# Inputs awaited one by one in five products, and two gate tiles moved into the waits of the attention

## The reference, cut to what matters

```python
def swiglu(x, w_in, w_out):
    gate, up = jnp.split(x @ w_in, 2, axis=-1)
    return (jax.nn.silu(gate) * up) @ w_out

def token_mixer(h, ...):
    z_hy, q, k, v, gates = jnp.split(h @ w_in, SPLITS, axis=-1)
    y_hy = hyena_branch(z_hy, ...) @ w_hy_out
    ...
    o = diff_attention(q, k, v, lam)
    o = rmsnorm(o, subln_g) * (1.0 - lam_init)
    y_da = o.reshape(B, L, D_ATTN) @ w_da_out
    g_hy, g_da = jnp.split(jax.nn.sigmoid(gates), 2, axis=-1)
    return (g_hy * y_hy + g_da * y_da) @ w_o
```

## Time and profile before

| | |
|---|---|
| time, median of 3 | 1986.11 us |
| the profiled execution | 1985.95 us, span 1984.1 us |
| PE busy | 1781.3 us (90%), granted clock 0.941 on average |
| DVE, ACT, POOL busy | 850.5, 310.7, 111.3 us |
| gates | 734.03 to 784.2 us |
| attention | to 859.9 us |
| head norm and `daout` | to 905.65 us |
| experts | from 1544.05 us |

### The profile page before, as it was taken

How to read it: one execution, slowest core, us unless ns; L and a number is a source line. 1 busy time by engine, 2 the same in 40 slices (tenths; PEclk the granted TensorE clock), 3 DMA queues, 4 the chain that set the end, 5 groups by cost and what they waited for, 6 DMA issues and landing times.

```text
span 1984.1 us, 29568 instructions
## 1 busy us (share of the span) xinstructions
PE 1781.3 (90%) x12188; PEld 1373.0 (69%) x12188; DVE 850.5 (43%) x1728; ACT 310.7 (16%) x707; POOL 111.3 (6%) x120
## 2 busy tenths in 40 slices
PE   6999999999999999999999999999999866666765
PEld 2788888888884878669999998888778321121212
DVE  4766666964442066734675236633433100000001
ACT  2200000010210112412111114212322100000000
POOL 2000000010100010000000002602001000000000
PEclk9999999999999999989999999989999887787778
DMA  8333444965442114116545863100359899999996
GB/s 362 131 130 129 137 136 158 353 219 193 149 149 85 64 57 157 43 64 234 186 167 172 292 215 115 43 23 24 130 219 395 348 433 432 427 431 431 433 433 291
DMA packets 46756, 426.08 MB, mean 215 GB/s; under 512 B 5331, under 2 KB 5940, under 8 KB 15548
## 3 DMA queue, kind: packets, MB, share of 16 engines
q1 hardware_dynamic: 37008, 386.97, 50.5%
q10 hardware_dynamic: 9644, 37.59, 5.3%
HBM read 423.49 MB, written 1.05 MB: 214 GB/s over the span
## 4 chain that ended last, share of the span: by engine, by line
PE 30%; DMA 19%; DVE 3%; POOL 2%; issue 1%; ACT 1%; SPq 0%; DVEq 0%; POOLq 0%; ACTq 0%
DMA arena<-experts_ring_dram 19%; PE bank L957 14%; PE bank L1132 6%; PE bank L1516 3%; PE bank L1800 2%; PE bank L1348 1%; DVE arena L2960 0%; PE bank L1619 0%; PE bank L1667 0%; PE bank L1398 0%; POOL rstd L868 0%; DVE rstd L2340 0%; PE bank L1710 0%; POOL arena L932 0%; PE bank L1593 0%
## 5 line engine op out<-in xcount | busy, mean ns | idle before, releaser
L957 PE MATMUL bank<-arena 128*128 128x256 f32 (+2 forms) x3296 | 624.8, 351 | 6.7 <-DVE arena L2811 1.9
L957 PEld LDWEIGHTS bank<-arena 128*128 128x128 f32 x3296 | 532.4, 192 | 92.0 <-issue 34.7
L1800 PE MATMUL bank<-arena 128*32 128x512 f32 x1400 | 230.3, 817 | 132.6 <-DMA arena<-experts_ring_dram 131.8
L1800 PEld LDWEIGHTS bank<-arena 128*32 128x32 f32 x1400 | 61.5, 143 | 294.7 <-issue 294.6
L1081 PE MATMUL bank<-arena 128*128 128x256 f32 x880 | 194.0, 379 | 0.0
L1081 PEld LDWEIGHTS bank<-arena 128*128 128x128 f32 x880 | 167.3, 190 | 22.9 <-issue 0.5
L1132 PE MATMUL bank<-arena 128*128 128x128 f32 x1512 | 169.2, 275 | 0.0
L1132 PEld LDWEIGHTS bank<-arena 128*128 128x128 f32 x1512 | 169.1, 192 | 0.1
L3151 DVE TENSOR_TENSOR arena<-arena,bank 128x512 f32<-128x512 f32 x8 | 5.5, 687 | 229.9 <-PE bank L1800 229.9
L2504 DVE SCALAR_TENSOR_TENSOR arena<-arena 128x1024 f32<-128x1024 f32 x56 | 68.4, 1221 | 0.0
L1516 PE MATMUL bank<-arena 64*64 64x64 f32 x2048 | 62.2, 221 | 0.8 <-POOL arena L932 0.5
(11 more groups left out here) (416 smaller groups left out, 1921.9 us busy)
## 6 DMA issues: line engine op xcount, KB each, us to landing
arena<-dense_dram SPq DMA_DIRECT2D x167, 1024.0 KB, 4.9
arena<-experts_ring_dram SPq DMA_DIRECT2D x41, 4096.0 KB, 26.9
arena<-ada_rest_dram ACTq DMA_DIRECT2D x56, 512.0 KB, 5.2
arena<-experts_dram SPq DMA_DIRECT2D x19, 1024.0 KB, 8.8
arena<-ada_head_dram SPq DMA_DIRECT2D x8, 1024.0 KB, 23.0
arena<-experts_dram SPq DMA_DIRECT2D x8, 512.0 KB, 9.8
arena<-tokens_dram ACTq DMA_DIRECT2D x1, 2048.0 KB, 20.0
arena<-experts_ring_dram SPq DMA_DIRECT2D x1, 2048.0 KB, 23.9
```

Source lines behind the costliest of these rows:

```text
L957: ins = mm(out, lhsT=w, rhs=rhs(k), start=k == 0, stop=k == k_tiles - 1)
L1800: ins = mm(ps[banks[half]][32 * e:32 * e + 32, :], lhsT=lhs[:, 2 * kp + par, CAP * e:CAP * e + CAP], rhs=slab[e][par][:, half * 512:half * ...
```

## The change

1. A `product` can be given a function `arrived`, called before each of its blocks. The first product of `ffn1_out` and of `ffn2_out` waits for all but the last two hidden tiles before block 0 and for these two before blocks 20 and 21. The first product of `daout` waits for bank k // 2 of the head norm before block k. `gated_add` counts every tile in `mix_ready`, and the first product of `wo` and of `wout` waits for tile k before block k. The waits for the whole input are gone.
2. Gate tiles 14 and 15, before the eighth pair, are plain products of 8 matmuls over 256 tokens. `gate14` stands behind the first scores, in bank 7; ACT copies it out after the first head's exponentials. `gate15` stands in bank 6 round the head norm: 2 blocks before the sums of squares, 5 between the sums and the spreading, 1 behind it. ACT applies both sigmoids after the head norm's root, and then loads the root's table again by a small Sqrt. DVE waits for them before tile 6 of `daout`.
3. The weight slabs are laid out in the new order; their number is unchanged.

```diff
-          ("uspec", {0: 2, 1: 2, 2: 2, 3: 2}), ("v_end", _rot(4)), ("yinv", _rot(8)), ("gates", _rot(16)),
-          ("att", {0: 8, 1: 8, 2: 8, 3: 8, 5: 8, 6: 8, 7: 8}), ("onorm", {5: 1, 0: 1, 1: 1, 2: 1, 3: 1}),
+          ("uspec", {0: 2, 1: 2, 2: 2, 3: 2}), ("v_end", _rot(4)), ("yinv", _rot(8)), ("gates", {0: 4, 1: 4, 2: 3, 3: 3}),
+          ("gate14", {7: 1}),
+          ("att", {0: 8, 1: 8, 2: 8, 3: 8, 5: 8, 6: 8, 7: 8}), ("gate15", {6: 1}), ("onorm", {5: 1, 0: 1, 1: 1, 2: 1, 3: 1}),
...
-GATE_PAIRS = KD
+GATE_PAIRS = KD - 1
+HY_EARLY = 2
...
+                    if arrived is not None:
+                        arrived(k)
...
-                pe.wait_ge(in_hid, FT)
...
-                pe.wait_ge(sv_hid, SEVENS)
...
+            def last_hidden(made):
+
+                def arrived(k):
+                    if k == 0:
+                        pe.wait_ge(made, FT - 2)
+                    elif k >= FT - 2:
+                        pe.wait_ge(made, k + 1)
+                return arrived
...
-            hyena_out(range(2))
+            hyena_out(range(HY_EARLY))
             scores(0)
-            hyena_out(range(2, 5))
+            take(pe, "gate14", 7, 0)
+            product(ps[7][:, 0:T], KD, lambda k: h1[:, k, 0:T], full[7])
+            hyena_out(range(HY_EARLY, 5))
...
+            def gate15(lo, hi):
...
+                for k in range(lo, hi):
+                    w, first = st.block()
+                    ins = mm(ps[6][:, 0:T], lhsT=w, rhs=h1[:, k, 0:T], start=k == 0, stop=k == KD - 1)
...
+            gate15(0, 2)
             pe.wait_ge(osq_ready, 8)
             take(pe, "onorm", 5, 0)
...
             ins.then_inc(full[5], 1)
+            gate15(2, 7)
             pe.wait_ge(hr_ready, 1)
...
-            for b in range(4):
-                evacuated(pe, "onorm", b, 0)
-            tiles("daout", KD, KD, lambda k: oT[:, k, :])
-            pe.wait_ge(mix_ready, 1)
...
+            gate15(7, KD)
+            for t in range(KD):
+                take(pe, "daout", t % 4, t // 4)
+                product(ps[t % 4][:, 0:T], KD, lambda k: oT[:, k, :], full[t % 4],
+                        arrived=None if t else lambda k: evacuated(pe, "onorm", k // 2, 0))
...
+            def mixed(stage):
+
+                return lambda k: pe.wait_ge(mix_ready, KD * stage + k + 1)
+
+            def second_hidden(k):
+                if k == 0:
+                    pe.wait_ge(sv_hid, SEVENS - 2)
+                elif k >= FT - 2:
+                    pe.wait_ge(sv_hid, SEVENS - FT + k + 1)
...
+            got(act, "gate14", 7, 0)
+            A(gates[:, 2 * GATE_PAIRS, :], ps[7][:, 0:T], ACT.Copy).then_inc(evac[7], 1)
...
+            got(act, "gate15", 6, 0)
+            A(gates[:, 2 * GATE_PAIRS + 1, :], ps[6][:, 0:T], ACT.Sigmoid).then_inc(evac[6], 1)
+            A(gates[:, 2 * GATE_PAIRS, :], gates[:, 2 * GATE_PAIRS, :], ACT.Sigmoid).then_inc(gate_done, 1)
+            A(fh[0:HEADS, 2 * T:2 * T + 1], eps[0:HEADS, 0:1], ACT.Sqrt)
...
-                    settle()
+                    if n == 0 and t == KD - 2:
+                        evacuated(dve, "gate15", 6, 0)
+                        dve.wait_ge(gate_done, GATE_PAIRS + 1)
+                    if t:
+                        dve.wait_ge(mix_ready, KD * n + t)
+                    else:
+                        settle()
                     tt_(rt[:, 0:T], ps[t % 4][:, 0:T], gts[:, first + t, :], mult).then_inc(evac[t % 4], 1)
                     evacuated(dve, stage, t % 4, t // 4)
-                    ins = tt_(dst[:, t, :], dst[:, t, :], rt[:, 0:T], add)
-                    if t < KD - 1:
-                        do(ins)
-                ins.then_inc(mix_ready, 1)
+                    tt_(dst[:, t, :], dst[:, t, :], rt[:, 0:T], add).then_inc(mix_ready, 1)
```

More of the change, by code:

```diff
@@ L63 @@
 N_COLS = _at
-DENSE = [("ffn1_in", FT), ("ffn1_out", 22), ("z", 12), ("qk", 8), ("v", 4), ("gates", 8),
-         ("hyout", 4), ("daout", 4), ("wo", 8), ("ffn2_in", FT), ("ffn2_out", 22), ("rwkv", 18.5 + 12)]
+DENSE = [("ffn1_in", FT), ("ffn1_out", 22), ("z", 12), ("qk", 8), ("v", 4), ("gates", 7),
+         ("hyout_daout", 9), ("wo", 8), ("ffn2_in", FT), ("ffn2_out", 22), ("rwkv", 18.5 + 12)]
 N_DENSE = int(math.ceil(sum(n for _, n in DENSE)))
@@ L285, in lay_out @@
         *(blocks(g["w_out_2"][0]).reshape(-1, P, P) for _ in range(2))])
+    first_gates = blocks(w_in[:, 6 * D:])
+    hyout = blocks(g["w_hy_out"][0]).reshape(-1, P, P)
     dense = np.concatenate([
         slabs(f1), *(slabs(blocks(g["w_ff_out"][0, 0])) for _ in range(2)), slabs(blocks(w_in[:, :5 * D])),
-        wide(w_in[:, 5 * D:6 * D]), slabs(blocks(w_in[:, 6 * D:])), slabs(blocks(g["w_hy_out"][0])),
-        slabs(blocks(g["w_da_out"][0])), *(slabs(blocks(g["w_o"][0])) for _ in range(2)),
+        wide(w_in[:, 5 * D:6 * D]), slabs(first_gates[:2 * GATE_PAIRS]),
+        slabs(np.concatenate([hyout[:HY_EARLY], first_gates[-2], hyout[HY_EARLY:], first_gates[-1],
+                              blocks(g["w_da_out"][0]).reshape(-1, P, P)])), *(slabs(blocks(g["w_o"][0])) for _ in range(2)),
         slabs(ffn_in(g["w_ff_in"][0, 1])), *(slabs(blocks(g["w_ff_out"][0, 1])) for _ in range(2)), slabs(second)])
@@ L948, in _, with product @@
             st = Stream(pe, slab_loaded, slab_started, ring, RING)
-            def product(out, k_tiles, rhs, last_sem=None, norm=None):
+            def product(out, k_tiles, rhs, last_sem=None, norm=None, arrived=None):
                 for k in range(k_tiles):
@@ L1193, in _ @@
                 take(pe, "ffn1_out", t % 4, t // 4)
-                product(ps[t % 4][:, 0:T], FT, lambda k: x_then_ctx(t, k), full[t % 4])
+                product(ps[t % 4][:, 0:T], FT, lambda k: x_then_ctx(t, k), full[t % 4],
+                        arrived=None if t else last_hidden(in_hid))
                 first_norms(t)
@@ L1307, in _ @@
                 ins.then_inc(full[7], 1)
+            def gate15(lo, hi):
+                if lo == 0:
+                    take(pe, "gate15", 6, 0)
+                for k in range(lo, hi):
+                    w, first = st.block()
+                    ins = mm(ps[6][:, 0:T], lhsT=w, rhs=h1[:, k, 0:T], start=k == 0, stop=k == KD - 1)
+                    if first:
+                        ins.then_inc(slab_started, 1)
+                if hi == KD:
+                    ins.then_inc(full[6], 1)
+            gate15(0, 2)
             pe.wait_ge(osq_ready, 8)
@@ L1323, in _, with by_halves @@
                     ins.then_inc(full[b], 1)
[L1324 to L1328 removed]
+            gate15(7, KD)
[3 more added lines that the diff above has]
+                        arrived=None if t else lambda k: evacuated(pe, "onorm", k // 2, 0))
+            def by_halves(stage, k_tiles, src, after, arrived=None):
                 for t in range(2 * KD):
@@ L1331, in by_halves @@
                     take(pe, stage, t % 4, t // 4)
-                    product(ps[t % 4][:, 0:P], k_tiles, lambda k: src[:, k, o:o + P], full[t % 4])
+                    product(ps[t % 4][:, 0:P], k_tiles, lambda k: src[:, k, o:o + P], full[t % 4],
+                            arrived=None if t else arrived)
                     after(t)
+            def mixed(stage):
[5 more added lines that the diff above has]
+                    pe.wait_ge(sv_hid, SEVENS - FT + k + 1)
             def half_tiles(stage, norm, after):
@@ L1378, in shift_norms @@
                     stat_of_sum(12, P)
-            by_halves("wo", KD, mix, wo_norms)
+            by_halves("wo", KD, mix, wo_norms, mixed(0))
             ffn2_in()
-            by_halves("ffn2_out", FT, hid2, ffn2_out_norms)
+            by_halves("ffn2_out", FT, hid2, ffn2_out_norms, second_hidden)
             half_tiles("shift", 5, shift_norms)
@@ L1719, in wout_norms @@
                     route(0)
-            by_halves("wout", KD, mix2, wout_norms)
+            by_halves("wout", KD, mix2, wout_norms, mixed(1))
             affinities_out(0)
```

11 lines of the change are left out of this document (5 added, 6 removed).

## The result

| | before | changed |
|---|---|---|
| first comparison, median | 1986.65 us (1985.02 to 1989.47, 5 runs) | 1977.37 us (1973.49 to 1978.34, 5 runs) |
| ratio | | 0.9943, 95% interval [0.9927, 0.9959] |
| profiled execution | 1985.95 us, span 1984.1 | 1977.37 us, span 1975.5 |
| second comparison | 1988.51 us | 1972.6 us, ratio 0.9918 [0.9905, 0.9931] |
| third comparison | 1990.09 us | 1971.55 us, ratio 0.9917 [0.9895, 0.9938] |

Forecast were 1971.0 us, 1966 to 1977, faster by over 0.2%. The kernel is faster in all three comparisons, by 9.3, 15.9 and 18.5 us of the medians, 14.6 on average against the 15.0 forecast. The first median, the one that the forecast was made for, lies 6.4 us above the 1971.0 and 0.4 us above the range; the other two lie inside it. Why the first profile shows only 8.6 us of span is the question of the experiments.

A forecast was written before the change was run, and what follows sets the result against it. PE's stream of products was taken to bound the kernel up to about 1550 us, with the experts' weights behind it, started by PE. 4.94 + 6.27 + 4.8 - 1.0 = 15.0 off 1985.95 gave 1971.0 us, range 1966 to 1977.

The forecast's parts named there:

- First products: Waits before `ffn1_out`, `ffn2_out`, `wo` and `wout` go, 1.31 + 1.69 + 1.94: gain 4.94 us; new waits cost nothing.
- The eighth pair: Gates: the eighth pair of gate tiles goes, so the attention starts 6.27 us earlier.
- `gate14`: Behind the first scores: its 3.46 us are free; the first product with v still starts 14.35 us after these scores.
- The clock in the first heads: Attention: later idle time may bring a half-speed stretch into the first full head; bounds 0 and 3.4, taken as 1.0 us.
- Head norm: `gate15` fills waits round the sums; the clock falls once, for 5 us, costing 2.5: gain 4.8 us.
- first rival: The clock holds at the head norm, which gains 7.3, and costs nothing in the attention; 1967.4 us, chance 0.20.
- so this is also the forecast for the median: Sum's last step: the profiled run is 0.16 us below the median, so 1971.0 us is forecast for the median too.
- the clock is as bad as it can be: Rival: worst clock at head norm and in the attention, 4.94 + 6.27 + 0.8 - 3.4 = 8.6 gained; 1977.3 us, chance 0.10.
- No change: Rival: the gain is swallowed by the experts' stream of weights; about 1986 us, chance 0.03.
- Slower: Rival: `gate14` moves PE's rest into the first head, half clock persists, each head costs some 8 us; about 2032, chance 0.05.

The follow-up runs named there:

- e6: Changed kernel with gate tile 14 directly behind the seven pairs in place of behind the first scores; 1974.77 us, ratio 0.9932.
- e5: Kernel before with only the head norm's spreading padded with zeros from 8 to 128 rows of contraction; 1983.67 us, ratio 0.9974.
- e4: Changed kernel with the head norm's spreading padded with zeros from 8 to 128 rows; 1969.66 us, ratio 0.991; again beside the changed kernel 1971.84 us.
- e9: Changed kernel with the head norm's spreading made three times over, 24 matmuls of 8 rows; 1980.98 us, one run.
- e10: Changed kernel with the head norm's spreading made three times over and padded with zeros to 128 rows; 1974.02 us, one run.

## Why the prediction came out as it did

- **First products.** Forecast 4.94, measured 1.6 + 1.9 at the two feed-forward nets and 1.24 each at `wo` and `wout`, 6.0. The step was right and 1.1 us small: taking a wait away gave 0.2 to 0.3 us more than the listed wait. The added waits cost nothing to be seen; the prediction counts 28 of them, the kernel has 30 where there were 8, so 22.
- **The eighth pair.** Forecast 6.27, measured 6.3 (51.0 to 44.7).
- **`gate14`.** Free as worked out, to 0.01 us; e6 shows the 3.5 us that it costs directly behind the pairs.
- **The clock in the first heads.** Forecast 1.0. The stretch at 795 was 3.4 us and exposed: 3.21 us for scores that take 1.99, and 76.8 for 75.8 up to the sums. In other executions it fell away (75.8). The 6.8 us stretch of before was covered, so the price is 1.0 or 0. But the forecast put the risk down to `gate14`, and that is not shown: e6, with `gate14` ahead of the scores, and e5, whose attention is that of the kernel before, have a stretch of 3.4 us and the same 76.8. The size was met, its cause is open.
- **Head norm.** Forecast one fall, 5 us long, gain 4.8. Measured 62.1 - 55.6 = 6.5, less the 1.24 of `wo` 5.3; with a stretch of 6.8 in the second profile 3.7. At full clock (e4) it is 62.1 - 53.6 - 1.24 = 7.3, forecast 7.3. The choice between forecast and first rival hung on the 8 rows, and e9 and e10 show that they lose the clock. The one fall came, 3.4 or 6.8 us long in place of 5.
- Together the terms measured 6.0 + 6.3 - 1.0 + 5.3 = 16.5 us in the first profile (rounded), 15.0 forecast.
- **The part that failed** is the sum's last step, "so this is also the forecast for the median", and the width of the range: both treated everything outside the touched stages as fixed. It is not. The start was 1.9 us longer in the first profile, 1.2 of it a first transfer (PE waits 4.0 us for it in the profile before, 5.2 after), and the clock falls differently in untouched stages. The second block and the experts, first and third profile of the same changed kernel:

```profile
1185.30:1501.20 315.90, 303.81 (x3693) 259.36 (x3693) 144.15 (x241) 92.45 (x185) 62.31 (x51) 0.96 0.31 116
...
1533.30:1975.50 442.20, 285.54 (x1761) 97.86 (x1760) 32.77 (x57) 20.12 (x33) 0.00 (x0) 0.79 0.95 408
```

```profile
1184.50:1496.00 311.50, 299.01 (x3693) 254.21 (x3693) 144.23 (x241) 92.34 (x185) 62.01 (x51) 0.98 0.31 118
...
1528.20:1968.50 440.30, 278.61 (x1762) 95.45 (x1760) 32.78 (x57) 19.76 (x33) 0.00 (x0) 0.81 0.96 410
```

The same instructions take 4.8 us less of PE in the one than in the other. At the very end, the last expert's outputs and the last norm, first the first profile, then the third:

```profile
1960.75 3.78 PE L1884 MATMUL bank<-rstd,arena 128*128 128x256 f32 x8 [0.79 <-DVE arena L3210]
1964.32 2.94 PE L976 MATMUL bank<-sq,small 128*128 128x256 f32 x8
```

```profile
1955.42 1.99 PE L1884 MATMUL bank<-rstd,arena 128*128 128x256 f32 x8 [0.81 <-DVE arena L3210]
1957.78 2.40 PE L976 MATMUL bank<-sq,small 128*128 128x256 f32 x8 [0.37 <-ACT sq L1946]
```

Here half clock costs 1.8 us on the path that ends the run, in one profile of the kernel and not in the other. Of the rivals, "the clock is as bad as it can be" gave 1977.3, which is the first median, but its mechanism did not occur; the number was met by chance. That the mean of three comparisons lies so near the forecast is in part luck too: the terms were 1.5 us too small, and in the first profile the untouched stages took back 7.9. "No change" fell, since the experts started 1544.0 - 1533.3 = 10.7 us earlier and ended 8.6 earlier. "Slower" fell: from the first product with v at 793.42 to the last at 853.07 seven heads take 8.5 us each.

Open stays why the changed kernel's first comparison (9.3 us) and the later two (15.9 and 18.5) differ by so much: only one profile of each was read by stages. The later two ran on two different chips. The granted clock of the changed kernel's runs was 0.942 to 0.945 in the first comparison and 0.945 to 0.951 in the third, which points the right way, but the slowest run of the third, 1977.97 us, has 0.951, so it does not settle it.

## What to carry to other kernels

Sum a change over the stages that it touches, and compare stage by stage: here single terms were good to 0.5 us while a whole execution scatters by several. Put work into the wait that a dependency chain of other engines sets, not beside it, and count the clock as a second gain: a filled hole of 2.33 us was worth 1.2 to 2.9 us more, by which profiles are compared. Pad a contraction of few rows where the clock matters; from 8 to 128 rows it cost nothing here.

## What was unexpected of the hardware

- With eight rows of contraction PE was 100% busy and lost the clock all the same (e9: 17.1 us at half; e10, with 128 rows: none). I had expected the fall from one row of the trace, not that it would go on as long as such matmuls do.
- A long stretch at half clock under full business is not always a matter of small operands. In the second block of the first changed profile the clock is half for 17.1 us with PE busy for all of them, on matmuls of 64 rows, 64 columns or both:

```profile
1317.10:1334.20 17.10, 17.10 (x170) 16.16 (x172) 2.29 (x4) 2.41 (x7) 3.95 (x4) 0.50 0.00 1
```

```profile
1316.96 1.81 PE L1543 MATMUL bank<-arena 128*128 128x64 f32 x8 [1.45 <-DVE arena L3012]
1318.70 1.12 PE L1549 MATMUL bank<-sq,arena 64*128 64x64 f32 x8
...
1328.59 6.58 PE L1559 MATMUL bank<-arena 64*64 64x64 f32 x132
```

But the 64x64 matmuls of L1559, which fill the last third of this stretch, also fill 27 us a little earlier in the same profile, at full clock; and in the third profile of the same kernel the stretch itself is at full clock, behind a wait of 1.43 us in place of 1.45. First the earlier window, then the third profile's:

```profile
1256.00:1283.00 27.00, 27.00 (x928) 26.98 (x926) 13.06 (x19) 5.78 (x10) 9.85 (x8) 1.00 0.02 4
```

```profile
1317.10:1334.20 17.10, 16.54 (x418) 15.73 (x419) 4.82 (x7) 3.91 (x9) 8.05 (x7) 1.00 0.01 3
```

So the same matmuls ran at either level. What decides which is open; the half-speed stretch began behind the wait. Whether padding these would hold the second block at its lower times was not tried.
- A wait taken away is worth 0.2 to 0.3 us more than the profile lists for it (1.31 gave 1.6, 1.69 gave 1.9 to 2.0, 0.97 gave 1.24). More than half of this is in how the rows are drawn, not in the chip: where PE does not wait, a row of 256-column matmuls ends about 0.16 us after the next one begins (853.07 + 1.89 = 854.96, and the next starts at 854.80), and a wait, listed from the drawn end of the row before it, costs that overlap as well. The other 0.1 us is not explained.
